# A two-layer hybrid backbone on one core: loads, stores, modulation pieces and sums of the first MLP's second product in another order, gate products and the last token low parts on GpSimd

## The reference, cut to what matters

```
mod = split((silu(c) @ w_ada[layer] + b_ada[layer]), 6)      # the same for the context with c_ctx
a   = rms_norm(h, g[0]) * (1 + mod[1]) + mod[0]
h   = h + mod[2] * rms_norm(mixer(a), g[1])
f   = square(relu((rms_norm(h, g[2]) * (1 + mod[4]) + mod[3]) @ w_ff1)) @ w_ff2
h   = h + mod[5] * rms_norm(f, g[3])
```

## Time and profile before

| | us |
|---|---|
| median of 3 runs | 1658.23 (1657.61 to 1659.26) |
| profiled execution | 1659.68 |
| its span | 1657.9 |
| PE busy | 1576.1 (95%) |
| DVE busy | 1283.9 (77%) |
| ACT busy | 846.7 (51%) |
| POOL busy | 156.8 (9%) |
| DMA | 220.95 MB, mean 133 GB/s |

### The profile page before, as it was taken

The page is one execution under the profiler, slowest core; times in us unless marked ns, Lnnn a source line. Parts: engine busy times, 40 slices in busy tenths (PEclk is TensorE's granted clock), DMA queues, the critical chain, the costliest instruction groups (busy, mean ns, idle before and its releaser), DMA issues.

```text
span 1657.9 us, 24945 instructions
## 1 busy us (share of the span) xinstructions
PE 1576.1 (95%) x9392; PEld 1362.2 (82%) x9392; DVE 1283.9 (77%) x2047; ACT 846.7 (51%) x1515; POOL 156.8 (9%) x171
## 2 busy tenths in 40 slices
PE   7999999999999999969999999889999999999997
PEld 4999888778778999967888777878877778888886
DVE  5889787686689788868889677775785778787778
ACT  5433476774374554545444565214664665444442
POOL 1000275331000000000000000002441000000000
PEclk9999999999999999999999999989999999999999
DMA  8533430014224455585853313433122132322221
GB/s 347 188 124 134 130 87 21 21 52 178 102 99 175 184 216 210 185 323 200 296 202 96 127 53 131 152 124 97 56 77 102 53 126 102 106 105 96 104 99 51
DMA packets 55990, 220.95 MB, mean 133 GB/s; under 512 B 6208, under 2 KB 19392, under 8 KB 41024
## 3 DMA queue, kind: packets, MB, share of 16 engines
q1 hardware_dynamic: 55872, 219.37, 37.6%
HBM read 181.33 MB, written 27.26 MB: 126 GB/s over the span
## 4 chain that ended last, share of the span: by engine, by line
PE 47%; DVE 13%; ACT 5%; DMA 5%; issue 4%; SPq 0%; DVEq 0%; ACTq 0%
PE ps L1827 12%; PE ps L1460 8%; PE ps L1462 8%; PE ps L1461 8%; PE ps L1633 2%; PE ps L1803 2%; PE ps L1606 2%; DMA raw<-in_w_ff 2%; DMA mod_raw<-in_w_ada_t 1%; ACT whi L2632 1%; PE ps L1584 1%; DVE ada_junk L3370 1%; DVE wlo L3620 1%; PE ps L1594 1%; DVE hs L3680 1%
## 5 line engine op out<-in xcount | busy, mean ns | idle before, releaser
L1460 PE MATMUL ps<-whi,ahi 128*128 128x256 f32 (+1 forms) x496 | 150.5, 303 | 4.3 <-DVE wlo L2955 2.4
L1461 PE MATMUL ps<-wlo,ahi 128*128 128x256 f32 (+1 forms) x496 | 148.0, 298 | 0.0
L1462 PE MATMUL ps<-whi,alo 128*128 128x256 f32 (+1 forms) x496 | 147.8, 298 | 0.0
L1827 PE MATMUL ps<-whi,tok_hi 128*128 128x512 f32 x336 | 133.0, 396 | 15.6 <-DVE tok_lo L3690 15.3
L1462 PE MATMUL ps<-ahi,wlo 128*128 128x512 f32 (+2 forms) x368 | 139.6, 379 | 0.0
L1460 PE MATMUL ps<-ahi,whi 128*128 128x512 f32 (+1 forms) x336 | 129.6, 386 | 4.0 <-ACT stage L2436 2.5
L1827 PE MATMUL ps<-whi,tok_lo 128*128 128x512 f32 x336 | 131.5, 391 | 0.0
L1827 PE MATMUL ps<-wlo,tok_hi 128*128 128x512 f32 x336 | 131.5, 391 | 0.0
L1461 PE MATMUL ps<-alo,whi 128*128 128x512 f32 (+1 forms) x336 | 128.8, 383 | 0.0
L3370 DVE SCALAR_TENSOR_TENSOR ada_junk<-mod_raw,silu_rows 128x1024 bf16<-128x1024 f32 x80 | 97.6, 1220 | 29.2 <-DMA mod_raw<-in_w_ada_t 27.2
L2666 ACT ACTIVATE whi<-down_land 128x1024 fp32r<-128x1024 f32 x56 | 59.3, 1058 | 107.9 <-PE ps L1827 101.2
(11 more groups left out here) (362 smaller groups left out, 4351.5 us busy)
## 6 DMA issues: line engine op xcount, KB each, us to landing
raw<-in_w_ff SPq DMA_DIRECT2D x48, 1024.0 KB, 4.8
tok_in<-token_rows SPq DMA_DIRECT2D x56, 384.0 KB, 3.0
mod_raw<-in_w_ada_t SPq DMA_DIRECT2D x16, 1024.0 KB, 7.3
down_land<-in_w_ff SPq DMA_DIRECT2D x32, 512.0 KB, 6.1
token_rows<-hs SPq DMA_DIRECT2D x40, 384.0 KB, 3.1
raw<-in_w_ada_t SPq DMA_DIRECT2D x12, 1024.0 KB, 4.8
mod_raw<-in_w_ada_t SPq DMA_DIRECT2D x24, 512.0 KB, 4.5
raw<-in_w_in_odd SPq DMA_DIRECT2D x9, 1024.0 KB, 4.9
```

The source lines that it names most:

```text
L1460: pe.matmul(dst, lhs[0], rhs[0], start=first, stop=False)
L1461: pe.matmul(dst, lhs[0], rhs[1], start=False, stop=False)
L1462: return pe.matmul(dst, lhs[1], rhs[0], start=False, stop=last)
L1827: ins = pe.matmul(dst, x_[m % 4][:, k, a], w_[:, k, :], start=first and not chained and k == 0 and j == 0, stop=last and k == 1 and j == 2 ...
```

## The change

It moves steps within the hand-written sequences of SP, ACT, DVE, and gives to POOL work that DVE did: the low parts of the token parts m = 50 to 55, the gate products of the first MLP's output, and the normalisation of tile 2. The index tables (`sq_list`, `NORM_READY`, `mod_value`) follow. A third buffer for halves of modulation units is added. The core of the diff:

```diff
@@ SP: straight
-                    if r == R_OUT0 + 2:
+                    if r == R_OUT0 + 3:
                         for j in range(2, 4):
                             sp.wait_ge(s_ada, pieces_before(j - 1))
+                            modulation_pair(j)
@@ SP: ff_in_phases
                         weight_block(0, "b11")
-                        weight_block(0, "b21")
...
                         token_part(0)
                         token_part(1)
-                        weight_block(1, "b11")
-                        weight_block(0, "b12")
-                        weight_block(0, "b22")
+                for name in ("b12", "b22"):
+                    weight_block(0, name)
+                for name in ("b11", "b12", "b22"):
+                    weight_block(1, name)
                 store(7, "a22")
-                weight_block(1, "b21")
...
+                for name in ("b11", "b12", "b22"):
+                    weight_block(2, name)
                 token_part(2)
                 token_part(3)
-                weight_block(2, "b12")
...
-                weight_block(3, "b21")
-                for name in ("s3", "s1", "s2", "a12", "s4"):
-                    store(7, name)
-                modulation_unit(MOD_UP)
-                modulation_unit(MOD_UP + 1)
+                for name in ("b11", "b12", "b22"):
+                    weight_block(3, name)
+                for c in range(4):
+                    weight_block(c, "b21")
                 for m, (name, c) in enumerate(DOWN_PARTS):
                     if m + 4 < len(DOWN_PARTS):
                         token_part(m + 4)
...
+                    if m == 1:
+                        for block_ in ("s3", "s1", "s2", "a12"):
+                            store(7, block_)
+                    elif m in (3, 5):
+                        modulation_unit(MOD_UP + (m - 3) // 2)
+                    elif m == 6:
+                        store(7, "s4")
@@ SP: input_loads and modulation_half
-                    if u < 5:
-                        continue
-                    for _ in range(2 if u == 5 else 5):
+                    for _ in range({3: 3, 6: 3, 7: 4, 8: 14}.get(u, 0)):
                         modulation_half(k)
...
-                if k < 2:
+                if k < 3:
                     sp.wait_ge(s_res, RES["01"] + NT)
+                    sp.wait_ge(s_tg, tg_index["pre10", KT - 1, 0] + 1)
                 else:
-                    sp.wait_ge(s_ada, pieces_before(MOD_DOWN) + k - 1)
+                    sp.wait_ge(s_ada, pieces_before(MOD_DOWN) + (k - 2 if k < 17 else k - 1))
@@ ACT
-                        normalize("pre10", 2, (4, 5))          # ahead of unit 1's copies out of PSUM
...
+                    if (layer, u) == (1, 1):
+                        normalize("pre10", 3, (4, 5))          # behind them
...
                 down_hi(0)
+                down_hi(1)
                 tokens_hi(0)
                 finish("c12", 7)
-                down_hi(1)
                 tokens_hi(1)
@@ POOL
+            def gate_columns(t, part, n=512):
+                c0 = 512 * part
+                pool.wait_ge(s_sq, sq_index["post01", t, part] + 1)
+                pool.tensor_tensor(xn[:, t, c0:c0 + n], xn[:, t, c0:c0 + n], gate01[:, 0 if t < NTL else 1, c0:c0 + n],
+                                   ALU.mult).then_inc(s_gated, 1)
...
+            for m in range(TOKENS_BY_POOL, len(DOWN_PARTS)):       # 50 to 55
+                pool.wait_ge(s_dthi, m + 1)
+                pool.wait_ge(s_dtlo, m)
+                pool.tensor_tensor(tok_lo[m % 4][:, :, :], tok_in[m % 4][:, :, :], tok_hi[m % 4][:, :, :].bitcast(F32),
+                                   ALU.subtract).then_inc(s_dtlo, 1)
+                if m == 52:
+                    wait_groups_before(pool, tg_index["gate01", 0, 1] + 1)
+                    for t in range(NTL):
+                        gate_columns(t, 1)
+            for t in range(NTL):
+                gate_columns(t, 0)
+                if t == 3:
+                    pool.wait_ge(s_rstd, NORM_READY["pre10"] + 1)
+                    pool.tensor_scalar(xn[:, 2, :], h[:, 2, :], norm_rstd[:, 10:11], 1.0, ALU.mult, ALU.mult).then_inc(s_xn, 1)
+            wait_groups_before(pool, tg_index["gate01", 1, 1] + 1)
+            for t in (4, 5):
+                gate_columns(t, 0, D)
@@ DVE: input_projection
-                    if layer == 1 and u >= 2:
-                        for _ in range(4 if u < 5 else 3):
+                    if layer == 1 and u in (1, 2):
+                        process_odd(u - 1)
+                    if layer == 1:
+                        for _ in range({2: 3, 3: 3, 4: 4, 5: 1, 6: 4}.get(u, 0)):
                             modulation_step()
...
-                    if layer == 1 and u in (1, 2, 4):
-                        process_odd({1: 0, 2: 1, 4: 4}[u])
+                    if (layer, u) == (1, 4):
+                        process_odd(4)
+                    if (layer, u) == (1, 6):
+                        for _ in range(9):
+                            modulation_step()
@@ DVE: output_projection
-                    for _ in range(8):
+                    for _ in range(12):
                         modulation_step()
                 split_lo(w0 + 2)
                 if layer == 0:
-                    for _ in range(8):
+                    for _ in range(4):
@@ DVE: ff_in_phases, chunk 1
-                    if c == 1:
-                        halves_lo("t3")
-                        halves_lo("t4")
-                    part_lo("p7", c)
+                    if c > 1:
+                        part_lo("p7", c)
                     token_sum_of(c - 1, "s3")
...
-                    modulation_step()
+                    if c > 1:
+                        modulation_step()
                     add_block(c, "c11")
+                    if c == 1:
+                        halves_lo("t3")
+                        part_lo("p7", c)
                     part_lo("p3", c)
-                    modulation_step()
+                    if c == 1:
+                        halves_lo("t4")
+                    else:
+                        modulation_step()
@@ DVE: ff_in_phases, second product
-                    tokens_lo(m)
-                    if m == 2:
+                    if m < TOKENS_BY_POOL:
+                        tokens_lo(m)
+                    if m == 4:
                         token_sum_of(7, "s4")
-                    if name == "p1":
-                        down_sum_of("t1", c)
-                    elif name == "p3":
-                        down_sum_of("t3", c)
-                        down_sum_of("t2", c)
+                    if m % 28 in range(2, 6):
+                        down_sum_of("t1", 4 * (m // 28) + m % 28 - 2)
+                    if m % 28 in range(5, 9):
+                        down_sum_of("t3", 4 * (m // 28) + m % 28 - 5)
+                        down_sum_of("t2", 4 * (m // 28) + m % 28 - 5)
```

More of the change, by code:

```diff
@@ L232, in build @@
                    for i, where in enumerate((A + 12 * KB, A + 20 * KB, B + 8 * KB, A + 30 * KB, H))]
-        mod_raw += [place(f"mod_raw{5 + i}", [P, D], F32, C + (24 + 4 * i) * KB) for i in range(2)]
+        mod_raw += [place(f"mod_raw{5 + i}", [P, D], F32, where) for i, where in enumerate((C + 24 * KB, C + 28 * KB, B + 8 * KB))]
         down_at = (1152, C + 16 * KB, C + 32 * KB, C)
@@ L560, in build @@
                 sq_list += [(post, t, 1) for t in range(nt)] + [(post, t, 0) for t in range(3)]
-                sq_list += [(pre, 0), (post, 3, 0), (pre, 1), (pre, 2), (pre, 3), (post, 4, 0), (post, 5, 0)]
+                sq_list += [(post, 3, 0)] + [(pre, i) for i in range(4)] + [(post, 4, 0), (post, 5, 0)]
             elif post[5] == "0":
@@ L686, in mod_slot, with half_slot, mod_value @@
                 return 2
-            return 3 + (j - MOD_UP) % 2 if j < MOD_DOWN else 5 + mt
-        def mod_value(j):
+            return 3 + (j - MOD_UP) % 2 if j < MOD_DOWN else half_slot(2 * (j - MOD_DOWN) + mt)
+        slot_of_half = [5 + k % 3 for k in range(15)] + [5 + (k - 15) % 2 for k in range(15, 24)]
+        def half_slot(k):
+            return slot_of_half[k]
+        def mod_value(j, mt):
             if j < 4:
@@ L3834, in ff_in_phases @@
                             copy_group(("gate01", 1, half))
+                    if m == 55:
+                        add_sum(12, "c11", "q22", 2)
                 post, pre = "post01", "pre10"
[L3836 removed]
+                assert gated[0] == GATED_BEFORE, gated[0]
+                gated[0] += 10
+                settled = lambda t: dve.wait_ge(s_gated, GATED_BEFORE + 5 + t)
                 back = lambda i: dve.wait_ge(s_hback[i], 16)
[L3838 removed]
                 post_root(post, 0, 3)
[L3840 to L3841 removed]
+                add_sum(13, "c21", "q43", 0)
                 back(0)
[L3843 to L3848 removed]
+                for t in range(3):
+                    settled(t)
+                    residual(post, t)
```

(8 more changed lines are left out.)

78 lines of the change are left out of this document (23 added, 55 removed).

## The result

| | before | changed |
|---|---|---|
| median, us | 1658.74 (4 runs) | 1630.82 (4 runs, 1629.78 to 1634.09) |
| ratio, 95% interval | | 0.9836 (0.9819 to 0.9853) |
| the same, measured once more | 1657.79 (9 runs) | 1628.11 (5 runs), 0.9829 (0.9816 to 0.9843) |
| profiled execution / span | 1659.68 / 1657.9 | 1634.09 / 1631.6; second 1626.4 / 1624.3 |

The change gains 27.9 us, in the second measurement 29.7. The prediction was 1620, so 10.8 us of the expected 38.6 are missing: 1630.8 lies 2.8 us outside the forecast's own range (1613 to 1628) and well inside the wider one (1604 to 1640). The first profile is of the slowest of the four executions; the second shows which of its waits repeat.

The account below looks back on a forecast made before the run. TensorE, in work for 95% of the span, was taken as the bound, so only its waits and half-speed time could be won. The terms summed to 38.6 us, giving 1620 us, own range 1613 to 1628, wider range 1604 to 1640.

Parts of the forecast that it names:

- A: Output projection: wait for the first quarter of a weight's low part goes, with its slow clock; gain 6.8 us.
- B: First product, chunk 1: wait for the snapshot goes as work is taken out ahead of c11; gain 6.5 us.
- C: Start of the second product: waits for token low parts shrink, with DMAs the bound; gain 9 us, bounds 4 and 17.
- D: Close of layer 0: VectorE and GpSimd serialise, so normalised tiles come later; loss 2 us, bounds minus 6 and plus 4.6.
- J: Attention's start: nine last modulation pieces, 2.7 us apiece, delay the first scores' maxima; loss 4 us, bounds 0 and minus 10.
- E: Near 1005 us: wait for copies out of PSUM goes because ScalarE makes them first; gain 3.2 us.
- F: Near 1053 us: waits for a rotary token and a low part go as process_odd(1) begins earlier; gain 7.4 us.
- G and H: Near 1097 and 1108 us: waits for a rotary token and the last unit's low part go; gains 7.7 and 4.0 us.
- Rival 2: Gains of C and J mostly given back and D costs 6 us: gain 24 us, time 1635; chance 22%.
- Rival 1: VectorE and GpSimd run side by side and the DMAs lead: gain 52 us, time 1606; chance 15%.
- rival 3: Moved steps miss their deadlines in F and G, and C gives 4: gain 21 us, time 1638; chance 6%.
- rival 4: Nine last modulation pieces become the bound, 7.5 us or more apart: slower than before, 1666 at 8.5 us; chance 3%.

Follow-up runs that it names:

- number 1: Kernel before with only the 12 and 4 modulation pieces, the later load of their third unit and the new chunk 1 order; 0.9951 of before.
- number 2: Changed kernel with chunk 1's four modulation pieces and all that follow moved one unit later; 0.9826 of before.
- number 3: Changed kernel with ScalarE's down_hi(1) back behind the first token copy and the finish of c12; 0.9836 of before.
- number 4: Changed kernel with the four b21 blocks issued one each behind token parts 5 to 8 instead of ahead of token part 4; 0.9812 of before.
- number 5: Changed kernel with number 3 and number 4 together, and the last chunk's s4 token sum with its store four parts later; 0.9780 of before.
- number 6: Changed kernel with the last six token low parts back on VectorE, gate products and one normalisation staying on GpSimd; 0.9830 of before.
- number 7: Changed kernel with the last six token low parts and all ten gate products back on VectorE; 0.9816 of before.
- number 8: Changed kernel with the fourth input unit split before the last four context slices, TensorE awaiting the slices only at the unit's context tiles; 0.9820 of before.
- number 9: Changed kernel without the last nine modulation pieces and their loads; 0.9806 of before.

## Why the prediction was near, and what failed in it

At every place that the prediction named, the wait went or came as it said; the sum was 38.6 us for 28 to 30. A and B, C, D, J and the two new losses were tested by kernels of their own; E to H rest on the rows of the profiles.

- **A and B** were right to 0.1 us in the changed kernel and to 0.3 in number 1.
- **B's last sentence failed**: "the next deadline (p6 of chunk 2) had 5.5 us of slack and keeps about 2". That was the wrong deadline. The pieces moved to the end of chunk 1 stand ahead of `c11` of chunk 2 as well, VectorE has only three gaps of 0.8 to 1.1 us from there to 548, and TensorE comes 13 us earlier by A and B. The snapshot of chunk 2 had no such slack: 4.5 us in both profiles, 3.2 in number 1, where the clock stayed full behind the wait; number 2 takes the wait away. I had looked at the next consumer of what was moved past, not at the same consumer one chunk on.
- **C, 9**, measured 6.6 and 9.1, and 8.1 on the mean over seven profiles of kernels that leave it alone: the size was right to 1 us. The late parts were 0 and 4 to 5 (6 in some), as forecast, for the reasons given: b11(1), token part 4 behind the b21 blocks, and the s4 sum (numbers 3 to 5).
- **D, -2**, measured -3.6 and -2.4. By the lock the rows are as predicted: in the time of before (TensorE's gain at 940 us added) the last residual ends at 973.9 and the tiles stand at 977.9, for 973.4 and 978. Where the loss comes from was not: "four residuals and four gate products stand in one line" costs little. With the low parts back on VectorE and the gate products still on GpSimd (number 6) they stand at 971.7 and 975.8, where before had 970.8 and 975.8, and without any gate product there (number 7) hardly earlier, at 971.5 and 975.6. The loss is the low parts of GpSimd, 2.2 us; the rest of the -3.6 and -2.4 goes with the clock behind the tiles. The Trainium skill (SBUF — State Buffer, Who interferes with whom) says that the lock is held for a whole instruction, and that VectorE takes it with two SBUF inputs or in a two-port mode. That a step on 128x3 took 1.21 us beside gate products of 1.26 us (3.77 for three) agrees; the step shown has one input, so only the second half of the rule would cover it, and no run here tells that apart.
- **E and F**: E brought 4.2 for 3.2 and F 8.2 for 7.4, and between them stand 4.3 us that the sum has not (2.3 and 2.4 in numbers 5 and 3, where the clock stayed full behind a wait of 2.1 us there). That the third unit's low part "must also be early" was carried through, the fourth's not: its high part waits for the context slices and these for `process_odd(0)`. TensorE, now without the wait for the copies, arrives before it (numbers 7 and 8). What E won was given back whole.
- **G and H, 11.7**: 12.3 and 11.5.
- **J, -4**: -5.5 and -2.1, on the mean -3.6 over the nine profiles of kernels on the changed order that leave it alone. Right in kind (number 9) and size; "2.7 us apiece" was 2.9 in the first profile.
- **The rivals.** Rival 2's 1635 lies nearer to the measured 1630.8 than the forecast's 1620, but not by its way: C was not given back, nor did D and J cost 6 and 10. Rival 1 fell with the lock, which is in the rows; rival 3's deadlines of F and G held; rival 4 was far off: it needed pieces 7.5 us apart.

So two deadlines that became binding only because TensorE came to them sooner cost 8.7 to 8.9 us in the two profiles. Both are one step behind a gain that I counted in full. That this is nearly the whole of the missing 9 to 11 us is in part luck: in the first profile all other stretches together stand 3.4 us under the forecast (C, D and J 5.5 under, E and F 1.9 over), in the second 3.7 over, and only on the mean do they even out.

## What to carry to other kernels

When a wait goes, carry the bound engine's new, earlier time through every following step of the engine that feeds it, not only to the next consumer: in a loop written out by hand, the same step of the next iteration. Before several gains are added, list each feeder's slack at each deadline and subtract what has been won ahead of it. When several repairs are tested together, read each one's share at its own place: in number 5 the token copy only moved its wait from part 0 to part 2, as it had alone, and the time came from the other two.

## What the runs showed of the hardware

**The same wait does not cost the same clock.** Windows from the restart behind a wait, with the granted clock (of full 2.4 GHz) behind the busy times. The snapshot at 551, waits of 2.64, 2.65 and 2.65 us, in the first and second profile of the changed kernel (there the window begins 0.4 us behind the restart) and in number 1:

```profile
551.43:556.00 4.57, 4.57 (x17) 4.57 (x18) 3.64 (x5) 2.55 (x3) 0.00 (x0) 0.63 0.32 116
```

```profile
551.09:556.00 4.91, 4.91 (x22) 4.91 (x21) 4.42 (x6) 2.10 (x3) 0.00 (x0) 0.65 0.45 159
```

```profile
551.46:556.00 4.54, 4.54 (x26) 4.54 (x27) 3.61 (x5) 2.55 (x3) 0.00 (x0) 1.00 0.32 114
```

TensorE had idled equally long and did the same work before, and ran partly at 1.2 GHz in two of them and not in the third. The stretch costs 4.5 us in the one case and 3.2 in the other. Of the eleven profiles with this wait (2.6 to 2.7 us), the first 5 us behind it had a clock of 0.66 in five and of 1.00 in six. Behind the wait of 3.7 us for the normalised tiles it was 0.50 in the first profile of the changed kernel, 0.66 in the second, and 1.00 in numbers 3 and 8, where the wait was as long (3.68 and 3.65). My sum took the clock of each restart as given by the wait; it is worth 1 to 2 us either way at each (an estimate from these stretches), which may be some of the 4 to 6 us by which executions of the changed kernel differ.

**An engine beside another pays in the short operations too.** Three steps on 128x3 that follow each other in the first profile (the first is 946.69 above, the others at 947.94 and 949.18) took 1.21 us each, where the same steps take 0.17 alone, and each ended within 0.03 us of a gate product of GpSimd. So a chain of small steps can pay a whole GpSimd product for each. Not all of VectorE's work is held: the additions `xn<-xn,ps`, with one input in PSUM, took 0.7 us each at 940.74 and 941.52, while GpSimd made a low part.
